# Root-mean-square statistics of the first layer, with tokens on partitions

## The reference

```python
def rmsnorm(x, g):
    x32 = x.astype(jnp.float32)
    y = x32 * lax.rsqrt(jnp.mean(x32 * x32, axis=-1, keepdims=True) + EPS)
    return (y * g.astype(jnp.float32)).astype(x.dtype)

def trunk_layer(l, x, cond, ...):
    mod = jax.nn.silu(cond) @ w_ada[l] + b_ada[l]
    shift, scale, gate = jnp.split(mod[:, None, :], 3, axis=-1)
    h = rmsnorm(x, norm_pre[l]) * (1 + scale) + shift
    proj = h @ w_in[l]
    ...
    x = x + gate * rmsnorm(o @ w_out[l], norm_post[l])
    return x, k, v
```

## Time and profile before

| | us |
|---|---|
| median of 3 runs | 1130.21 |
| lowest, highest | 1129.47, 1130.28 |
| profiled execution | 1126.79 |
| its span (first to last instruction) | 1125.0 |
| TensorE busy | 1095.3 (97%) |
| VectorE busy | 703.7 (63%) |
| ScalarE busy | 423.1 (38%) |
| mean granted TensorE clock | 0.992 |

### The profile page before, as it was taken

How to read it: one execution, slowest core, us unless ns; L and a number is a source line. 1 busy time by engine, 2 the same in 40 slices (tenths; PEclk the granted TensorE clock), 3 DMA queues, 4 the chain that set the end, 5 groups by cost and what they waited for, 6 DMA issues and landing times.

```text
span 1125.0 us, 13506 instructions
## 1 busy us (share of the span) xinstructions
PE 1095.3 (97%) x5334; PEld 877.2 (78%) x5334; DVE 703.7 (63%) x1003; ACT 423.1 (38%) x684; POOL 33.5 (3%) x66
## 2 busy tenths in 40 slices
PE   5899999999999999999999899999999999999997
PEld 3566677887878887788888788888888888888885
DVE  5545555776767787699955655476756766343335
ACT  3423333443456343243334852223332323243332
POOL 0000010000000000000020000000000000000000
PEclk8999999999999999999999999999999999999999
DMA  9799876564535667677885243545445654444423
GB/s 359 321 360 354 325 265 253 197 236 157 212 154 233 257 231 297 236 254 272 323 309 200 75 150 134 184 155 200 163 178 186 222 202 173 168 142 140 145 80 112
DMA packets 39326, 242.27 MB, mean 215 GB/s; under 512 B 4784, under 2 KB 4896, under 8 KB 13408
## 3 DMA queue, kind: packets, MB, share of 16 engines
q1 hardware_dynamic: 29232, 190.85, 44.7%
q0 software_dynamic: 7344, 46.29, 11.4%
q10 hardware_dynamic: 2688, 4.26, 1.4%
HBM read 237.67 MB, written 3.72 MB: 215 GB/s over the span
## 4 chain that ended last, share of the span: by engine, by line
PE 93%; DVE 4%; DMA 1%; ACT 1%; issue 0%; DVEq 0%; ACTq 0%; SPq 0%
PE bank L899 26%; PE bank L901 26%; PE bank L900 26%; PE bank L943 2%; PE bank L1023 2%; PE bank L964 1%; DVE x_sums L1473 1%; PE bank L1087 1%; PE bank L1039 1%; PE bank L1002 1%; DMA raw_first<-in_ada_first 1%; PE bank L1046 1%; DVE x L1433 1%; PE bank L853 1%; PE bank L851 1%; PE bank L852 1%
## 5 line engine op out<-in xcount | busy, mean ns | idle before, releaser
L899 PE MATMUL bank<-w_hi,h_op 128*128 128x512 f32 x1116 | 451.9, 405 | 3.5 <-DVE h_op L1604 2.9
L901 PE MATMUL bank<-w_hi,h_op 128*128 128x512 f32 x1116 | 436.2, 391 | 0.0
L900 PE MATMUL bank<-w_lo,h_op 128*128 128x512 f32 x1116 | 435.8, 391 | 0.0
L1400 DVE TENSOR_TENSOR w_lo<-raw,w_hi 128x1024 fp32r<-128x1024 f32 x224 | 273.8, 1223 | 204.2 <-ACT w_hi L1128 203.9
L1128 ACT ACTIVATE w_hi<-raw 128x1024 fp32r<-128x1024 f32 x224 | 235.2, 1056 | 266.1 <-PE bank L901 249.1
L899 PEld LDWEIGHTS bank<-w_hi,h_op 128*128 128x128 f32 x1116 | 209.8, 188 | 64.1 <-issue 20.5
L901 PEld LDWEIGHTS bank<-w_hi,h_op 128*128 128x128 f32 x1116 | 209.6, 188 | 45.5
L900 PEld LDWEIGHTS bank<-w_lo,h_op 128*128 128x128 f32 x1116 | 210.2, 188 | 39.8
L899 PE MATMUL bank<-w_hi,o_low 128*128 128x512 f32 x192 | 75.8, 395 | 0.0
L901 PE MATMUL bank<-w_hi,o_low 128*128 128x512 f32 x192 | 74.9, 390 | 0.0
L900 PE MATMUL bank<-w_lo,o_low 128*128 128x512 f32 x192 | 74.8, 390 | 0.0
(11 more groups left out here) (203 smaller groups left out, 873.8 us busy)
## 6 DMA issues: line engine op xcount, KB each, us to landing
raw<-in_w_in SPq DMA_DIRECT2D x68, 1024.0 KB, 5.6
dot_raw<-in_ada_tiles POOLq DMA_DIRECT2D x32, 1024.0 KB, 5.1
raw<-in_w_out SPq DMA_DIRECT2D x32, 1024.0 KB, 4.9
raw_first<-in_ada_first SPq DMA_DIRECT2D x25, 1024.0 KB, 8.8
raw<-in_ada_groups SPq DMA_DIRECT2D x16, 1024.0 KB, 6.6
raw<-in_ada_halves SPq DMA_DIRECT2D x16, 1024.0 KB, 4.7
raw<-in_w_in SPq DMA_DIRECT2D x24, 512.0 KB, 6.8
dot_raw<-in_ada_first SPq DMA_DIRECT2D x7, 1024.0 KB, 5.7
```

Source lines behind the costliest of these rows:

```text
L899: pe.matmul(out, operand(layer, kind, 0, k, t), hi, start=k == begin, stop=False)
L900: pe.matmul(out, operand(layer, kind, 0, k, t), lo, start=False, stop=False)
L901: last = pe.matmul(out, operand(layer, kind, 1, k, t), hi, start=False, stop=k == end)
L1400: dve.tensor_tensor(w_lo[:, half % WRING, :, :].rearrange("p k n -> p (k n)"), src, hi, ALU.subtract)\
```

## The change

The squares of a part are summed on DVE by adding halves of the part to each other, then its tiles, and no longer by a reduction. TensorE now takes the tile of squares as the stationary operand and two columns of ones as the moving one: nine products, three parts for each of three token tiles, put the totals of 128 tokens on 128 partitions, one number each. ACT takes the root of 128 x 3 numbers, DVE the reciprocal and scales three identities by it (`x_diag`). Three products of the tile of ones and these diagonals put each token's factor on every partition, and ACT copies them to `root`. The one-element root of ACT stands behind all squares. In the timetable the entries `x_sum` go, `x_column` and `x_scale` stand between the two halves of the first modulation products, `x_spread` behind them, and `x_norm` for tile 0 behind `first_cols`. `x_scale`, the semaphore that releases `x_norm`, is now given by ACT's copy.

```diff
     pre(0, "x_total")
     pre(0, "warm", OPENING[0][0], 12)
-    pre(0, "x_sum", 0)
     pre(0, "first_ada", 0, 0)
-    pre(0, "x_sum", 1)
-    pre(0, "x_sum", 2)
+    pre(0, "x_column")
+    pre(0, "x_scale")
     pre(0, "first_ada", 0, 1)
-    pre(0, "x_scale")
+    pre(0, "x_spread")
+    pre(0, "first_cols", 0)
     pre(0, "x_norm", 0)
-    pre(0, "first_cols", 0)
     pre(0, "x_norm", 1)
...
-            def sum_x(i):
-
-                if i == 0:
-                    pe.wait_ge(cleared, 3)
-                pe.wait_ge(x_summed, i + 1)
-                ins = pe.matmul(acc(KEPT, 0)[:, 0:NT], ones[:, :], x_sums[:, i, :], start=i == 0,
-                                stop=i == len(X_PARTS) - 1)
-                if i == len(X_PARTS) - 1:
-                    ins.then_inc(x_totalled, 1)
+            def column_x():
+
+                pe.wait_ge(cleared, 3)
+                pe.wait_ge(x_summed, len(X_PARTS))
+                for t in range(TOKS):
+                    for i in range(len(X_PARTS)):
+                        last = pe.matmul(acc(KEPT, 0)[:, 2 * t:2 * t + 2], x_sums[:, i, t * P:(t + 1) * P], ones[:, 0:2],
+                                         start=i == 0, stop=i == len(X_PARTS) - 1)
+                last.then_inc(x_totalled, 1)
+
+            def spread_x():
+
+                for t in range(TOKS):
+                    pe.wait_ge(x_inverted, t + 1)
+                    last = pe.matmul(acc(KEPT, 1)[:, t * P:(t + 1) * P], ones[:, :], x_diag[:, t, :],
+                                     start=True, stop=True)
+                last.then_inc(x_spread, 1)
...
                     act.activation(x_sq[:, a:b, :], x_t[:, a:b, :], ACT.Square).then_inc(x_squared, 1)
-                    if i == 0:
-
-                        act.activation(junk[:, 0:1], eps[:, :], ACT.Sqrt)
+
+                act.activation(junk[:, 0:1], eps[:, :], ACT.Sqrt)
                 act.wait_ge(x_totalled, 1)
-                act.activation(root[:, :], acc(KEPT, 0)[:, 0:NT], ACT.Sqrt, scale=1.0 / D, bias=eps[:, :])\
-                    .then_inc(x_root, 1)
+                act.activation(stat[:, 6, :], acc(KEPT, 0)[:, 0:2 * TOKS].rearrange("p (t n) -> p t n", n=2)[:, :, 0],
+                               ACT.Sqrt, scale=1.0 / D, bias=eps[:, :]).then_inc(x_root, 1)
+                act.wait_ge(x_spread, 1)
+                act.activation(root[:, :], acc(KEPT, 1)[:, 0:NT], ACT.Copy).then_inc(x_scale, 1)
...
                         dve.wait_ge(x_squared, i + 1)
-                        dve.tensor_reduce(x_sums[:, i, :], x_sq[:, a:b, :].rearrange("p k t -> p t k"), AX.X, ALU.add)\
-                            .then_inc(x_summed, 1)
+                        half = (b - a) // 2
+                        then_own(dve.tensor_tensor(x_sq[:, a:a + half, :], x_sq[:, a:a + half, :], x_sq[:, a + half:b, :],
+                                                   ALU.add))
+                        one = dve.tensor_tensor(x_sums[:, i, :], x_sq[:, a, :], x_sq[:, a + 1, :], ALU.add)
+                        if half == 3:
+                            then_own(one)
+                            one = dve.tensor_tensor(x_sums[:, i, :], x_sums[:, i, :], x_sq[:, a + 2, :], ALU.add)
+                        one.then_inc(x_summed, 1)
                 elif what == "x_scale":
                     dve.wait_ge(x_root, 1)
-                    dve.reciprocal(root[:, :], root[:, :]).then_inc(x_scale, 1)
+                    then_own(dve.reciprocal(stat[:, 7, :], stat[:, 6, :]))
+                    for t in range(TOKS):
+                        dve.tensor_scalar(x_diag[:, t, :], ident[:, :], stat[:, 7, t:t + 1], None, ALU.mult)\
+                            .then_inc(x_inverted, 1)
```

More of the change, by code:

```diff
@@ L487, in hybrid_step @@
         x_sums = in_area("x_sums", [len(X_PARTS), NT], 0)
+        x_diag = in_area("x_diag", [TOKS, P], len(X_PARTS) * NT + P)
         ones = in_area("ones", [P], len(X_PARTS) * NT)
@@ L543, in hybrid_step @@
         x_totalled = sem("x_totalled")
+        x_inverted = sem("x_inverted")
+        x_spread = sem("x_spread")
         x_normed = sem("x_normed")
@@ L1105, in _ @@
                         warm_products(*e[1:])
-                    elif e[0] == "x_sum":
-                        sum_x(e[1])
+                    elif e[0] == "x_column":
+                        column_x()
+                    elif e[0] == "x_spread":
+                        spread_x()
         @block.scalar
```

## The result

The changed kernel takes 1123.04 us (median of four executions, 1121.32 to 1124.47). The kernel before, on the same chip, takes 1129.84 (four executions, 1128.84 to 1130.28). The ratio is 0.994, with a 95% interval of 0.9923 to 0.9958. So it is faster by 6.8 us, and the interval allows 4.7 to 8.7. Forecast were 4.7 us and 1125.5, with a range from 1123.3 to 1127.9.

A forecast was written before the change was run, and what follows sets the result against it. DVE's sums were taken to bound the first 20 us and a queue order the next six. A 5.9 us gain at full clock less 1.2 for the clock gave 4.7: 1130.2 - 4.7 = 1125.5 us, range 1123.3 to 1127.9.

The forecast's parts named there:

- What bounds: Kernel opening: DVE's sums bound the first 20 us, a queue order the next six.
- Sums: DVE in the opening: additions replace three reductions (10.91 us), so the last sum ends 4.2 us earlier than 19.90.
- Table: ACT in the opening: table load and one-element root move behind the squares, 12.9 to 14.4, covered by the wait for totals.
- Column totals: TensorE behind the last sum: 18 fp32 passes at 0.12, 2.2 us plus 0.1, from 15.75 to 18.1, none hidden.
- Root, inverse, spread: After 18.1: root 0.29, reciprocal 0.16, three identities at 0.29, spread 0.72 or 1.36, ACT copy 0.58; 20.45 at full clock.
- the charge of 1.2: Opening from about 18 us: 1.2 of a possible 1.8 us deducted from the 5.9 us gain for a clock fall.
- First weight product: End of the opening chain: starts at 23.95 at full clock or 25.75 if the clock falls, against 29.85 before.
- Transfers: DMA ahead of the load issued at 33.21: over five empty microseconds, so a shift of 4.7 fits and the opening moves whole.
- half clock and dear columns: Rival, opening: clock falls before the column passes, which take 4.1 us; gain only 2.4, 1127.8 us; chance 0.13.
- Swallowed: Rival, loads after the opening: they can't start earlier, TensorE waits for them, time stays 1130.2 us; chance 0.07.
- doesn't do what it says: Rival, opening: sums ready early but weight or modulation loads, say, release x_norm; gain 0 to 2, about 1129.2; chance 0.04.
- slower: Rival, opening: TensorE regains full clock late; half clock until 40 us loses 7.1 and gives 1133.2 us; chance 0.04.

The follow-up runs named there:

- split columns: Changed kernel with each x part's column products issued once that part is summed, against the changed kernel; 1120.36 us (0.993 to before), repeated 1120.92 (0.9926).

## Why the prediction was right or wrong

*What bounds.* Right. DVE's sums were the bound of the first 20 us, and what was won at the first weight product was found again at 180 us: 3.2 and 2.9 in the changed kernel, 7.5 and 7.4 in the one with split columns (173.6 us).

*Sums.* Right in size: 4.2 us by forecast, 4.2 in the trace (15.73 against 19.90). 1.36, 0.56 and 0.95 were measured for 1.36, 0.55 and 0.96.

*Table.* Right, it costs and gains nothing by itself (0.9998). Beside the additions its place matters: in the old one the last sum ends at 16.27 in place of 15.73.

*Column totals.* Mis-sized by the clock. At full clock twelve passes take 1.50, 0.125 each with the end of the last, near the 0.12 taken. Inside the block they start 0.11 apart (ten between 15.52 and 16.52), so the trace agrees with the 0.107 of the Trainium skill ("TensorE: Matmul & The Clock Gate", LDWEIGHTS), and the end of the block is what the 0.12 has over it. But in all three profiled executions of the changed kernel the clock fell during these passes, which then took 3.40, 2.56 and 2.85 for the 2.3 of the forecast. I had allowed the fall for the steps behind them, at 18, not inside them. That the nine wait for the last sum, which the forecast noted, was the larger loss: issued by part they cost 0.9 to 1.3 us behind the last sum in three traces, in place of 2.7 to 3.5, and the kernel gained another 2.6, second only to the additions.

*Root, inverse, spread.* Right: 0.27, 0.18, 0.68 for three identities, the copy 0.49 for 0.58. The modulation products (1.86) hid the inverse, and modulation products and spread ran at half clock, as the charge of 1.2 assumed in part. From the end of the totals to the first weight product all three traces take 7.38, for 7.65 by the forecast with the fall; the one trace at full clock there takes 5.61, for 5.85.

*First weight product.* Forecast 23.95 at full clock and 25.75 with the fall; measured 26.65, 25.71 and 26.29. The middle of the forecast, 25.15, was about 1.1 too early. The charge should have been the full 1.8, and the passes took 0.6 more on average than the 2.3.

*Transfers.* Hardly a loss, as forecast: 3.2 us at the first weight product are 2.9 at the attention, 4.1 are 4.2 and 3.6 are 3.8 in the other two traces. The empty stretch of the DMA engines shrank from about 6.4 us to 4.3 (by the shares between 26 and 35), so by less than the shift, as the loads behind it moved forward too. The bound of 5.6 us on the shift was met only for a while: with split columns the load behind the first modulation products is waited for (5.87 us from issue to use), 1.3 us of idle time at 30.3 against 0.7 before, but a later wait is shorter by as much (0.6 at 54.2 against 1.3), and at 173.6 us the whole 7.4 us are still there.

*The total.* Here is the step that failed, the sum 1130.2 - 4.7 = 1125.5, by its first term. It took the level of the kernel before from three executions, 1130.21; 75 executions have a mean of 1128.6, 1.6 lower. And its range held the unknown prices but not the scatter of executions, which reaches some 3 us to each side and moves a median of four by up to a microsecond. Of the 2.5 us between 1125.5 and 1123.04, the level makes up 1.6, the gain 0.4 (5.1 for 4.7) and the chance of four executions 0.5 (fifteen have a mean of 1123.5). From 1128.6 the same sum gives 1123.9 and the same range begins at 1121.7. Against the four executions of before taken beside it (1129.84) the parts would be 0.4 of level and 2.1 of gain; the larger sample speaks for the first account.

That the gain of 5.1 lies so near to 4.7 is in part luck: the first weight product came only 3.6 early, as the column totals and the clock were priced too low, and 1.5 came from elsewhere.

The 3.6 are those by which the first weight product is early on average (26.2 of three traces against 29.8 of two). The profiled executions themselves differ by 3.5 (means of 1123.9 and 1127.4), so the traces show no gain beyond the opening, and the other 1.5 lies in executions that have none. The mean granted clock of all executions went from 0.9922 to 0.9935. If half of a clock cycle missing is time lost to TensorE, that is 0.0013 x 1124 = 1.5 us, and 3.6 + 1.5 = 5.1. This is arithmetic on rounded averages, part of it is already in the 3.6 or counts time in which TensorE waited anyway, and no run isolates it. In 71 executions of the kernel before whose clock is known, lower clock goes with longer time (1129.7 on average for 17 at 0.991, 1127.6 for 15 at 0.993), but 11 at 0.994 give 1127.9, so clock is not the only thing that differs. What else does stays open.

Of the rivals, *half clock and dear columns* was the nearest to what the profiles show: its first product was put at 27.4, against 26.65 at the latest. But the forecast's own case with the fall, 25.75, is nearer to two of the three traces, and the passes cost 3.40/18 = 0.19 at most, under the 0.2 that was to show it wrong. The Trainium skill ("TensorE: Matmul & The Clock Gate", The HAM clock gate) says the clock is throttled unless activity releases it; the trace of the changed kernel agrees, the clock being back at 23.3 only after TensorE had been busy from 15.87 on. How small products count stays open, as the traces go both ways: with the column products by part TensorE was busy nearly without a pause in two executions, and the clock held in one and fell at 16.3 in the other. *Swallowed*, *doesn't do what it says* and *slower* are excluded by 0.994 and by the early attention.

## What to carry to other kernels

Products that wait for the last of several inputs should be issued as each input comes: the nine small products in a block behind the last sum lay on the path with all their 2.6 to 3.4 us, and issued by part they left 0.9 to 1.3 of them there. Price such a block at half clock too: in all three traces the clock fell inside it. When a start-up chain is shortened, look at what TensorE does in the new gap, since idle time ahead of the first dense products may be paid again at half clock in them; here eight more warm products covered it. And before a gain of half a percent is put against a median, see how far executions of the same kernel lie apart; here three were not enough to know the level within a microsecond.

## What the runs showed of the hardware

The same kernel has its clock fall at another moment or for another time in each execution: 18.1 to 28.3 and 18.5 to 25.3 in two executions of the kernel before, and 3.4 or 6.8 us at layer two. A longer fall cost nothing in that opening (first weight product at 29.85 and 29.81), where TensorE waits anyway, and 1.2 to 1.6 us at layer two, where it doesn't. A fall needs no idle time right ahead of it: with the column products by part it came once at 16.3, TensorE having paused for no more than 0.2 us since 8.1; its work from 13.1 on was column passes and modulation products with 32 weight columns. Products of fp32 with two moving columns and 128 weight columns take 0.125 us per pass at full clock and 3.97/18 = 0.22 at half, about the same as products with 128 moving columns (0.12 and 0.226); so here a very narrow product is as dear as one 64 times as wide. A reduction with a stride over tiles takes 1.8 ns for an element read (10.91 us for 6144), and the additions that take its place 6.55 us in all (9.18 to 15.73).
